# The rounded part and the remainder of each k tile side by side in h and in o

## The reference

```
h = rmsnorm(x, norm_g);  proj = h @ w_in            # 2048 -> 4*2048 + 16 + 6*2048
log_f  = log_sigmoid(f_logit + b_f)                 # 16 heads of 128
o_att  = softmax(q k^T / sqrt(128) + cumulated log_f, causal) @ v
y_att  = (o_att  * silu(z_att))  @ w_att_o          # 2048 x 2048
o_conv = gate_b * short_conv(gate_c * u)            # 3 taps along the tokens
y_conv = (o_conv * silu(z_conv)) @ w_conv_o         # 2048 x 2048
merged = sigmoid(m_att) * y_att + sigmoid(m_conv) * y_conv
out    = rmsnorm(x + merged @ w_out, final_gain)    # 2048 x 2048
```

## Time and profile before

| | |
|---|---|
| median of 3 runs | 1256.45 us (1256.13 to 1259.38) |
| span of the profiled execution | 1254.9 us; the fastest run shown is 1.2 us above it, the median 1.55 us |
| PE busy | 1238.4 us (99%) in 7977 matmuls |
| DVE, ACT, POOL busy | 797.0, 610.8 and 46.9 us |
| mean granted clock of PE | 0.998 of 2.4 GHz |
| matmuls over h and o | 2048 pairs of 512 and 256 columns (1536 over h, 512 over o); 1040 times three of 258 or 272 columns (h) |

### The profile page before, as it was taken

How to read it: one execution, slowest core, us unless ns; L and a number is a source line. 1 busy time by engine, 2 the same in 40 slices (tenths; PEclk the granted TensorE clock), 3 DMA queues, 4 the chain that set the end, 5 groups by cost and what they waited for, 6 DMA issues and landing times.

```text
span 1254.9 us, 21613 instructions
## 1 busy us (share of the span) xinstructions
PE 1238.4 (99%) x7977; PEld 1126.9 (90%) x7977; DVE 797.0 (64%) x870; ACT 610.8 (49%) x744; POOL 46.9 (4%) x50
## 2 busy tenths in 40 slices
PE   7999999999999999999999999999999999999997
PEld 6999999999998888889999999999999888888886
DVE  6756665566565655555777776776777666566544
ACT  6554444354345545443454543545445455454432
POOL 1000000000000000001011010110101000000000
PEclk9999999999999999999999999999999999999999
DMA  6865756655564665656464754646546466566663
GB/s 209 250 185 164 221 156 195 200 176 184 175 201 149 220 199 172 187 177 210 135 182 139 214 159 134 201 148 199 168 122 212 142 186 213 183 190 204 200 217 127
DMA packets 212948, 229.21 MB, mean 183 GB/s; under 512 B 7136, under 2 KB 205872, under 8 KB 212528
## 3 DMA queue, kind: packets, MB, share of 16 engines
q1 hardware_dynamic: 211712, 226.55, 58.6%
q10 hardware_dynamic: 1216, 2.38, 0.7%
HBM read 226.79 MB, written 2.11 MB: 182 GB/s over the span
## 4 chain that ended last, share of the span: by engine, by line
PE 97%; issue 1%; DMA 0%; ACT 0%; POOL 0%; DVE 0%; ACTq 0%; POOLq 0%; SPq 0%
PE ps L888 38%; PE ps L889 20%; PE ps L875 13%; PE ps L876 12%; PE ps L874 12%; DMA x_nat<-in_x 0%; PE ps L924 0%; PE ps L995 0%; PE ps L1005 0%; PE ps L1008 0%; PE ps L918 0%; POOL rstd L350 0%; PE ps L1007 0%; PE ps L1006 0%; PE ps L996 0%
## 5 line engine op out<-in xcount | busy, mean ns | idle before, releaser
L530 DVE TENSOR_TENSOR w_lo<-w_raw,w_hi 128x1024 fp32r<-128x1024 f32 x417 | 504.2, 1243 | 182.2 <-ACT w_hi L375 180.0
L375 ACT CAST w_hi<-w_raw 128x1024 fp32r<-128x1024 f32 x418 | 426.9, 1049 | 246.0 <-PE ps L889 96.0
L888 PE MATMUL ps<-h,w_hi 128*128 128x512 f32 x1536 | 542.4, 394 | 0.0
L889 PE MATMUL ps<-h,w_lo 128*128 128x256 f32 x1536 | 432.3, 281 | 0.0
L888 PEld LDWEIGHTS ps<-h,w_hi 128*128 128x128 f32 x1536 | 288.4, 188 | 65.0
L875 PE MATMUL ps<-h,w_hi 128*128 128x258 f32 (+1 forms) x1040 | 297.4, 286 | 0.0
L874 PE MATMUL ps<-h,w_hi 128*128 128x258 f32 (+1 forms) x1040 | 297.1, 286 | 0.0
L876 PE MATMUL ps<-h,w_lo 128*128 128x258 f32 (+1 forms) x1040 | 296.6, 285 | 0.0
L889 PEld LDWEIGHTS ps<-h,w_lo 128*128 128x128 f32 x1536 | 288.7, 188 | 0.0
L874 PEld LDWEIGHTS ps<-h,w_hi 128*128 128x128 f32 x1040 | 195.8, 188 | 0.7
L876 PEld LDWEIGHTS ps<-h,w_lo 128*128 128x128 f32 x1040 | 195.8, 188 | 0.0
(11 more groups left out here) (136 smaller groups left out, 641.6 us busy)
## 6 DMA issues: line engine op xcount, KB each, us to landing
w_raw<-in_w_in SPq DMA_DIRECT2D x322, 512.0 KB, 4.7
w_raw<-in_w_conv_o SPq DMA_DIRECT2D x32, 512.0 KB, 4.9
w_raw<-in_w_att_o SPq DMA_DIRECT2D x32, 512.0 KB, 5.1
w_raw<-in_w_out SPq DMA_DIRECT2D x32, 512.0 KB, 4.7
neg_cb<-neg_c_dram ACTq DMA_DIRECT2D x8, 272.0 KB, 3.2
x_nat<-in_x SPq DMA_DIRECT2D x4, 512.0 KB, 6.6
x_res<-in_x SPq DMA_DIRECT2D x1, 2048.0 KB, 10.5
out<-y SPq DMA_DIRECT2D x8, 256.0 KB, 2.9
```

The costliest lines, as they stand in the source:

```text
L375: nc.scalar.copy(w_hi[:, c % RING, :], w_raw[:, c % RAW, :]).then_inc(w_rounded, 1)
L530: nc.vector.tensor_tensor(w_lo[:, c % RING, :], w_raw[:, c % RAW, :], w_hi[:, c % RING, :].bitcast(F32), ALU.subtract).then_inc(w_split, 1)
L888: nc.tensor.matmul(dst, a_hi, b, start=start, stop=False)
L889: return nc.tensor.matmul(dst[:, HI, :], a_lo, b[:, HI, :], start=False, stop=stop)
```

## The change

`h` was `[P, 2, KT, TOK]`: a plane with the 16 HI tiles, then a plane with the 16 LO tiles. It becomes `[P, KT, 2, TOK]`: HI of k tile 0, LO of k tile 0, HI of k tile 1, and so on. `o` likewise. Every read and write of them gets its indices in the new order; nothing else is changed, and PE, POOL and SP issue the same instructions in the same order.

```diff
-    h = place("h", "h", [P, 2, KT, TOK], F32R)
-    o = place("o", "o", [P, 2, KT, SEQ], F32R)
+    h = place("h", "h", [P, KT, 2, TOK], F32R)
+    o = place("o", "o", [P, KT, 2, SEQ], F32R)
...
-                nc.scalar.activation(h[:, HI, k, :], ps[:, h_bank(k), 0:TOK], ACT.Copy,
+                nc.scalar.activation(h[:, k, HI, :], ps[:, h_bank(k), 0:TOK], ACT.Copy,
...
-                nc.scalar.copy(o[:, HI, bass.ds(i * 2, 2), :], prod2[:]).then_inc(o_rounded, 1)
+                nc.scalar.copy(o[:, bass.ds(i * 2, 2), HI, :], prod2[:]).then_inc(o_rounded, 1)
...
-                nc.vector.tensor_tensor(o[:, LO, bass.ds(i * 2, 2), :], prod2[:],
-                                        o[:, HI, bass.ds(i * 2, 2), :].bitcast(F32), ALU.subtract
+                nc.vector.tensor_tensor(o[:, bass.ds(i * 2, 2), LO, :], prod2[:],
+                                        o[:, bass.ds(i * 2, 2), HI, :].bitcast(F32), ALU.subtract
...
-                            last = wide_product(halves(bank + b), hi, lo, src[:, :, k, part],
+                            last = wide_product(halves(bank + b), hi, lo, src[:, k, :, part],
...
-                            last = product(ps[:, bank + b, 0:cols], hi, lo, src[:, HI, k, part],
-                                           src[:, LO, k, part], start=(k == 0), stop=(k == KT - 1))
+                            last = product(ps[:, bank + b, 0:cols], hi, lo, src[:, k, HI, part],
+                                           src[:, k, LO, part], start=(k == 0), stop=(k == KT - 1))
```

More of the change, by code:

```diff
@@ L586, in split_h @@
                 dve.wait_ge(h_rounded, k + 1)
-                nc.vector.scalar_tensor_tensor(out=h[:, LO, k, :], in0=ps[:, h_bank(k), 0:TOK],
-                                               scalar=chan[:, TAPS, k:k + 1], in1=h[:, HI, k, :].bitcast(F32),
+                nc.vector.scalar_tensor_tensor(out=h[:, k, LO, :], in0=ps[:, h_bank(k), 0:TOK],
+                                               scalar=chan[:, TAPS, k:k + 1], in1=h[:, k, HI, :].bitcast(F32),
                                                op0=ALU.mult, op1=ALU.subtract).then_inc(h_split, 1)
```

## The result

Over 21 runs each, the kernel before takes 1256.44 us (median) and the changed one 1258.58 us: ratio of the two 1.0017, 95% interval 1.0011 to 1.0023. One run of each took far longer (2806 and 6461 us) and is left out of the ratio. The changed kernel is 2.1 us slower, clear of zero but under the 0.3% of the prediction. The forecast was 1.0 us faster.

A forecast was written before the change was run, and what follows sets the result against it. PE's matmuls were taken to bound the kernel. Terms of -2.3 us (o), +1.3 (h wide pairs), 0 (h products) and 0 (writes) gave -1.0, so 1256.45 becomes 1255.4 us; own range 1253 to 1258, wide range 1250.5 to 1260.5.

The forecast's parts named there:

- Bound: Whole kernel: PE is 97% of the chain and never starved once running; only matmul start-to-start distances change the time.
- the writes: ACT and DVE writes to o in two runs of 256: hidden, 0; at most 1.3 us in ma without cover.
- o, wide pairs: 512 pairs over o in mc and ma become contiguous, 345.5 ns each: -2.3 us, bounds -0.6 and -3.4.
- One of the prediction's signs: o in the profile after: if mc is still near 353 ns, the layout is not what makes it dear.
- The clue: mc and ma read the same o addresses yet differ by 6.8 ns a pair, unexplained by the planes' distance alone.
- Rival 1: All matmul streams: distance does not depend on layout, so all terms 0 and 1256.45 us; chance 0.20.
- Rival 3: h's 1536 wide pairs enter the dearer pattern, +5.2 us, at most +4 to +5 with o halved, 1261 us; chance 0.16.
- h, wide pairs: 1536 pairs over h, changed block alignment: +0.8 ns a pair, +1.3 us, bounds -3.8 and +3.8.
- The rule behind the term: h's wide pairs: blocks starting 64 bytes past a multiple of 128 are dearer, about 5 ns a pair between k tiles.
- the prediction expected h's k tiles to stop alternating: h in the profile after: k tiles no longer alternate by 0.01 us.
- h, products: 1040 products of three matmuls over h: 0, bounds -2.6 and +2.6 us, no row for the sign.
- A flat distance: Skill's columns / 2.4 + 2.5 ns gap whatever the address: wide pair 325 ns before and after, change worth nothing.

The follow-up runs named there:

- e1: Kernel before with only o's HI and LO parts side by side, h kept in two planes: 1256.62 us, ratio 0.9998.
- e2: Kernel before with only h's HI and LO parts side by side, o kept in two planes: 1258.72 us, ratio 1.0016.
- e3: PE-only kernel, block left out: 24 rows of wide pairs, four layouts after six preludes; o 346.7 or 353.3 ns a pair in both its layouts.
- e7: Kernel before, layout untouched, plus one 16-column matmul on PE ahead of each o half of ma: 1259.04 us.
- e5: PE-only kernel, block left out: 38 rows at fixed HI/LO alignments (64/0: bytes past a multiple of 256) and shifted h tiles; 64/0 took 346.8 ns a wide pair.
- e6: Changed kernel with h moved up by 64 bytes and everything behind it by 256: 1254.01 us, ratio to the kernel before 0.9980.
- e9: PE-only kernel, block left out: h tiles side by side and in planes, shifted by 0 to 224 bytes; side by side at 96, 348.3 ns a wide pair.
- e11: Changed kernel with h and everything behind it moved up by 256 bytes: 1258.86 us, ratio to the kernel before 1.0022.
- e10: Kernel before, h in planes, with h moved up by 64 bytes and all behind it by 256: 1253.46 us, ratio 0.9978.

## Why the prediction was wrong

The time lies 2.1 us above the kernel before, not 1.0 us under it, and 0.6 us above the forecast's own range. That it lies within the wide range of 1250.5 to 1260.5 us says nothing for the mechanism.

- **Bound.** Right: PE alone, nothing else moved, the writes stayed hidden at 0.62 and 0.69 us.
- **o, wide pairs.** This is the step that failed. I took -2.3 us because the contiguous rows of the output product were "the nearest". They are nearest in shape only; they stand in a stream of equal 512-column matmuls, not between a 256 and a 256. Making o contiguous is worth 0 (e1), and o as a whole lost 1.4 us because ma's half changed pattern (e2, e3, e7). The bounds of the term, -0.6 to -3.4, excluded what happened, since I let the layout of o alone act on o. One of the prediction's signs did come true: mc stayed near 353, so the layout isn't what makes it dear. No sign watched for a dearer ma.
- **The clue.** The prediction saw that mc and ma read the same addresses at 353.4 and 346.6 ns and said that the distance between the planes can't explain it. It then used the difference only as something that the change might remove, not as something that it might bring to ma. Rival 1 named "the phase in which the loop begins" but priced it as if the change left the phase alone. Rival 3 had the dear pattern and its 6.8 ns a pair, in the wrong place: it put it into h's stream and halved the o term.
- **h, wide pairs.** +1.3 us forecast, +0.1 measured: the steady pattern in the changed kernel is 351.65 ns, 1.65 ns more than the 350.0 of before, but its first k tiles are cheaper than that, so that a half of mc comes to 350.6; and the z quarter (-0.5 us) and ma's h half (-0.4 us) had been dearer than 350.0. The rule behind the term, that 64-off starts are the dear ones, is refuted by 64/0 in e5 and by e6. Two places in the traces speak against it too. First k tiles 8 to 11 of an o half of mc before the change, then k tiles 8 to 11 of h in ma after it:

```profile
452.69 0.40 PE L888 MATMUL ps<-o,w_hi 128*128 128x512 f32 x1
...
453.39 0.40 PE L888 MATMUL ps<-o,w_hi 128*128 128x512 f32 x1
...
454.10 0.40 PE L888 MATMUL ps<-o,w_hi 128*128 128x512 f32 x1
...
454.81 0.40 PE L888 MATMUL ps<-o,w_hi 128*128 128x512 f32 x1
```
```profile
1144.67 0.40 PE L888 MATMUL ps<-h,w_hi 128*128 128x512 f32 x1
...
1145.39 0.39 PE L888 MATMUL ps<-h,w_hi 128*128 128x512 f32 x1
...
1146.08 0.40 PE L888 MATMUL ps<-h,w_hi 128*128 128x512 f32 x1
...
1146.80 0.39 PE L888 MATMUL ps<-h,w_hi 128*128 128x512 f32 x1
```

In o all tiles are aligned alike, and still its k tiles take 699, 710 and 711 ns in turn, a period of three (0.70, 0.71 and 0.71 us in the lines). And where the prediction expected h's k tiles to stop alternating, since all are now alike past a multiple of 128, they alternate more, by 713 and 693 ns (0.72, 0.69 and 0.72 us). So a cost that differs by k tile doesn't point at the alignment of that tile.

- **h, products.** 0 forecast, +0.85 us measured, within the bounds of 2.6. The sign for which there was no row is in e5: 359.4 ns a product side by side against 358.3 in planes at 258 columns, 376.7 against 375.0 to 375.8 at 272, after both preludes.
- **A flat distance.** The rule of the Trainium skill ("TensorE: Matmul & The Clock Gate", "Back-to-back issue gap") had no part in the sum; the traces have 26.6 ns (ma's o half before) to 36.7 ns (e9 at 160) over the columns in a wide pair, at one granted clock, by alignment and history, and so don't agree with it.

Shown: the effect comes from h's layout alone; o's distance is nothing; ma's o half can take either value at the same addresses; a 64-byte shift of h moves the patterns of both tiles. The patterns come with PE alone, and e2 and e11, on two chips, have every stage of the changed kernel within 0.02 us, so they are no chance of one execution. Argued, not shown: how h's layout brings ma's o half into the dear pattern. It fits that h in planes has two patterns and h side by side only one (e3): before, mc's o half follows h at 350.0 and ma's follows h at 352.5, and they differ; after, both follow the same h pattern and both take 352.8. Open: what inside TensorE holds the pattern; and no run here varied the weights' addresses on their own.

## What to carry to other kernels

Where matmuls bound a kernel at 99% as here, the layouts and shifts tried moved a wide pair by up to 7 ns of 350, and a stream can settle in one of several steady patterns, depending on what ran before it. Before costing such a change, look whether stages with equal addresses already differ: if they do, a change upstream can move them either way. A base shift of a tile by 32 to 96 bytes is a cheap thing to sweep with a PE-only kernel. Here 96 bytes were worth 6.2 us in the changed kernel, more than the layout cost (2.1 us), and 64 bytes were worth 3.0 us in the kernel before. The PE-only rows carried over for the wide pairs and not for the products, so the best shift has to be run in the kernel.

## What the hardware did that I had not expected

- Two steady patterns for one instruction stream: 346.7 and 353.3 ns a wide pair (512 and 256 columns with their weights), at the same addresses and a granted clock of 0.998 to 0.999; and 350.0 or 352.5 for h in planes.
- Two column blocks 16384 bytes apart cost what one run of 512 columns costs (e1; in e3 346.7 and 353.3 ns in both).
- In a PE-only stream (e5) all of 32/32, 64/0 and 192/0 bytes give the low value after both preludes, 192/192 the high one after both.
- Moving h and all tiles behind it by 256 bytes changes nothing (e11); moving h by 64 of these 256 bytes changes the kernel by 3.0 to 4.6 us (e10, e6).
